# First norm's modulation in a two-layer DiT block: columns in eight buffers, pairs of chunks side by side, reordered loads and weight shares

## The chip, the cores and the metric

The kernel runs on one core of one Trainium2 chip. The metric is the device time of one execution in microseconds (us), as the median of three runs. Engines are called PE (TensorE), DVE (VectorE), ACT (ScalarE), POOL (GpSimd) and SP (SyncE, which here only issues DMAs). Line numbers (L1359) are those of the kernel before, as the profile has them.

## The reference

What is computed is two layers of a transformer block on 256 latent and 256 context tokens of width 1024. Only its start matters here:

```python
mod  = silu(c)     @ w_mod[l] + b_mod[l]      # 6 x 1024 values: sh1, sc1, g1, sh2, sc2, g2
modc = silu(c_ctx) @ w_mod[l] + b_mod[l]      # the same for the context tokens
h  = rms_norm(x,  g_norm1[l]) * (1 + sc1)  + sh1
hc = rms_norm(xc, g_norm1[l]) * (1 + scc1) + shc1
y, yc = token_mixer(h, hc, ...)               # mLSTM, MLA and neighbourhood attention, merged
x = x + g1 * y
x = x + g2 * sqrelu_mlp(rms_norm(x, g_norm2[l]) * (1 + sc2) + sh2, w_ff1[l], w_ff2[l])
```

All is float32. `c` and `c_ctx` are single vectors, so the modulation is a product of a 1024-vector (two of them, latent and context) with a matrix of 1024 x 6144.

## The kernel before

Features lie on the 128 partitions in KC = 8 chunks, the 512 tokens on the free axis. A product in float32 is made as three products of rounded operands: each weight block and each activation is split into a high part (hH, wH, a rounded copy) and a low part (hL, wL, the rest), and PE does high*high, high*low and low*high. ACT makes the high parts of the weights (`high`, L831 to L841), POOL and DVE the low parts. A weight block lies in the ring `raw`, `wH`, `wL`, which has room for two of the 1 MiB blocks `ml`. For a block called shared, DVE does the first 5/8 of the low part (`share_ahead`, L1280 to L1291, 1280 columns) and POOL the last 3/8 (768 columns). Blocks ml 0 and ml 1 are shared.

The order of work is written out by hand: each engine has its own program, which it runs in order, and waits on semaphores. What lies ahead of the first projection:

- **Shift and gate values by DVE.** `mod(m)` (L1293) multiplies rows of w_mod with the broadcast silu(c) and sums along the free axis, four passes of 1024 elements for each 1 MiB of w_mod. The first four (MOD_START = 4) give the shift sh1 of layer 0. Two buffers hold the data, so the load of mod m waits until mod m-2 is done (L571).
- **Scale values by PE.** The scale sc1 of layer 0 is made by `columns(i)` (L2002): for each chunk i of the contraction, 0.5 MiB of w_mod (`p_modk`) is streamed against a stationary operand of two columns (latent, context) into two PSUM banks, rows 0 and 1. Five buffers hold the eight chunks (L392), so chunks 5, 6 and 7 wait until PE has read 0, 1 and 2 (L614). ACT copies the two rows out (L928 to L930, a bank at a time), PE turns them onto the partitions (L2036 to L2041), and DVE adds the bias (L1358 to L1360) and makes the gains (L1320).
- **Tokens.** PE transposes x and ctx (L2021 to L2026), ACT copies them to `x` (L922) and squares them (L889), PE sums the squares with a matrix of ones (L1999), ACT makes 1/rms by Ln and Exp (L901, L902).
- **The norm** (`norm` on DVE, L1323, and on ACT, L897). DVE scales chunks c and c+1 (`scaled`, L1335), ACT adds the shift and rounds (L910, L912), DVE makes the low part of the even chunk (L1344) and POOL that of the odd chunk (L718). DVE's scaling of chunk 5 waits for POOL's low part of chunk 1.
- **The first projection** (`leading`, L1894 to L1913). PE takes each chunk of h as soon as its low part is there, for three groups of weights in ml 0 and ml 1 (9 matmuls of 512 columns a chunk, 72 in all).

ACT's order is: squares, `ahead(-1)` (the high parts of ml 0 and ml 1, L927), the two copies of the scale rows (L928), the DMA that spills x, then Ln and Exp. DVE's order is: mod 0 to 3, `share_ahead(-1)` (its shares of ml 0 and ml 1, L1353), bias of the shift (L1356), the wait for the turned scale rows (L1357), two adds (L1359), two gains (L1320), the norm. SP's order of loads is:

```python
load_mod(0); ctx, x; load_columns(0); load_mod(1); load_columns(1..4)
load_mod(2); ml 0, ml 1; load_columns(5); load_mod(3); load_columns(6), (7); ml 2 ...
```

All these transfers go through one hardware queue, in order. ml 2 takes the place of ml 0, so its load waits for both halves of ml 0's low part (L562, L565).

Of the kernel before, what the change touches and what calls it, by code (L numbers as in the profile page):

```python
# [25 lines left out]
ALU = mybir.AluOpType  # L26
ACT = mybir.ActivationFunctionType
AX = mybir.AxisListType.X

D = 1024  # L30
# [6 lines left out]
P = 128  # L37
KC = D // P
# [19 lines left out]
R_G1, R_G2, R_BMOD, R_GOUT, R_GCQ, R_GCKV, R_GQ, R_GK, R_NGQ, R_NGK = (0, 8, 16, 64, 68, 71, 73, 74, 75, 76)  # L58
# [57 lines left out]
class Steps:  # L116
# [5 lines left out]
    def link(self, instruction):  # L122
        instruction.then_inc(self.sem, 1)
        self.n += 1
        self.eng.wait_ge(self.sem, self.n)
# [198 lines left out]
def build(nc, a, out):  # L324
    ctx = ExitStack()
    with ctx:
# [5 lines left out]
        def S(name):  # L332
            if name not in sems:
                phase, _, what = name.partition("_")
                base, hw = 0, name
                if what and phase[-1].isdigit():
                    kind = phase.rstrip("0123456789")
                    turn = 2 * int(phase[3]) + int(phase[4]) if kind == "nrm" else int(phase[-1])
                    hw = f"{kind}_{what}"
                    base = sum(signals(kind, t)[what] for t in range(turn))  # L340
                if hw not in handles:
                    handles[hw] = ctx.enter_context(nc.semaphore(hw))
                sems[name] = Sem(handles[hw], base)
            return sems[name]
# [14 lines left out]
        par = sb("par", [P, DEPTH, N_ROWS])  # L359
        modT = sb("modT", [P, DEPTH, 48, 2])  # L360
        gain = sb("gain", [P, KC, 2])
        cb = sb("cb", [P, 2, D])
        ccol = sb("ccol", [P, KC, 2])
# [10 lines left out]
        def view(at, *dims):  # L374
            n = int(np.prod(dims))
            v = arena[:, at:at + n]
            if len(dims) == 2:
                return v.rearrange("p (a b) -> p a b", a=dims[0])
            if len(dims) == 3:
                return v.rearrange("p (a b c) -> p a b c", a=dims[0], b=dims[1])  # L380
            return v

        x = view(0, KC, TOK)
        ident = const[:, C_ID:C_ID + P]
        flip = const[:, C_FLIP:C_FLIP + P]
        ones = const[:, C_ONE:C_ONE + P]
        bank = [ctx.enter_context(nc.psum_tensor("bank0", [P, 512], F32))]
# [2 lines left out]
        bank += [ctx.enter_context(nc.psum_tensor(f"bank{b}", [P, 512], F32)) for b in range(3, 8)]  # L390
        m_nd = pair[:, :].rearrange("p (t w) -> p t w", t=NTILE)
        k_raw = [view(at, D) for at in (12288, 13312, 14336, 6144, 7168)]  # L392
        k_row = gst[:, :, :].rearrange("p s t -> p (s t)")
        x_spill = nc.dram_tensor("x_spill", (P, KC, TOK), F32).ap()

# [161 lines left out]
        def _(sp):  # L557
# [10 lines left out]
            def load_mod(m):  # L568

                if m >= 2:  # L570
                    sp.wait_ge(*S("mod_done").at(m - 1))  # L571
                if m == MODS:
                    sp.wait_ge(*S("mg0_low").at(KC))
                l, pair = PAIRS[m]
                src = a["p_mod"][l][2 * pair:2 * pair + 2].rearrange("c p k -> p c k")
                sp.dma_start(mod_raw[:, m % 2, :, :], src).then_inc(S(f"mod_full{m % 2}").handle, 16)
# [31 lines left out]
            def load_all(name, l, js):  # L608
                for j in js:
                    load(name, l, j)  # L610
            def load_columns(i):

                if i >= len(k_raw):
                    sp.wait_ge(*S("k_done").at(i - len(k_raw) + 1))  # L614
                sp.dma_start(k_raw[i % len(k_raw)], a["p_modk"][i]).then_inc(S(f"k_full{i % len(k_raw)}").handle, 16)

            load_mod(0)
            for src, dst in ((a["ctx"], 0), (a["x"], 2)):
                sp.dma_start(xtok[:, dst:dst + 2, :], src[0].rearrange("(t p) d -> p t d", p=P)).then_inc(S("x_in").up(16), 16)
            load_columns(0)  # L620
            load_mod(1)
            for i in range(1, 5):
                load_columns(i)
            load_mod(2)
            load_all("ml", 0, range(2))
            load_columns(5)
            load_mod(3)
            load_columns(6)
            load_columns(7)
            for j in range(2, 7):  # L630
                load("ml", 0, j)
                if MOD_START + j - 2 < MOD_PROJ:
# [152 lines left out]
        def _(act):  # L785
            steps = Steps(act, S("act_step").handle)
            link = steps.link
# [138 lines left out]
                square(0, 0, 0, c)  # L926
            ahead(-1)  # L927
            for b in range(2):  # L928
                act.wait_ge(*(S("k_done").at(KC) if b else S("k_row").at(1)))
                act.activation(k_row[0:2, 512 * b:512 * b + 512], bank[b][0:2, :], ACT.Copy).then_inc(S("k_out").up(1), 1)  # L930
            act.wait_ge(*S("zeroed").at(1))
            for l in range(DEPTH):
                t0 = first_token(l)
# [5 lines left out]
                for j in range(7):  # L939
                    ahead(N["ml", l, j])  # L940
                    for b in range(2):
                        if j == 1:
                            src = full(u0 + j, b)[:, :].rearrange("p (a s t) -> p a s t", a=2, s=2)
                            for i in range(2):
                                for r in range(2):
                                    ins = act.activation(m_k[64 * r:64 * r + 64, 2 * b + i], src[64 * i:64 * i + 64, :, r, :], ACT.Copy)
# [45 lines left out]
                for it in range(2 * ML_H + 2):  # L992
# [4 lines left out]
                    h = it // 2 - 1  # L997
# [10 lines left out]
                for br in ("na", "mla"):  # L1008
# [5 lines left out]
                    if br == "mla":  # L1014
                        act.activation(l_t, small[:, :, 32:64], ACT.Square).then_inc(S(tag + "krs").up(1), 1)
                        exp_and_ln()
                        for j in range(2):
                            for b in range(2):
                                c = 2 * j + b
# [238 lines left out]
        def _(dve):  # L1258
            steps = Steps(dve, S("dve_step").handle)
            link = steps.link  # L1260
# [19 lines left out]
            def share_ahead(n):  # L1280

                while share_at[0] < reach(n):
                    m = share_at[0]
                    share_at[0] += 1
                    if not SHARED[m]:
                        continue
                    cut = cut_chunk(blocks[m][1]) * blocks[m][2]
                    dve.wait_ge(*S("w_high").at(2 * m + 1))
                    dve.tensor_tensor(flat(wL, m)[:, 0:cut], flat(raw, m)[:, 0:cut],
                                      flat(wH, m)[:, 0:cut].bitcast(F32), ALU.subtract)\  # L1290
                        .then_inc(S("w_share").handle, share_step(m))  # L1291
# [31 lines left out]
            def norm(l, which, t0):  # L1323
                tag = f"nrm{l}{which}_"
                sh = M_SH1 if which == 0 else M_SH2
                dve.wait_ge(*S(tag + "std").at(1))
                halves = [(s, lo) for s, lo in ((CTXS, 0), (LAT, CTX)) if lo >= t0]

                def scaled(c):

                    if c >= 4 and c % 2:
                        dve.wait_ge(*S(tag + "lowp").at((c - 3) // 2))
                    for s, lo in halves:
                        r = slice(lo, lo + 256)
                        dve.scalar_tensor_tensor(n_t[:, c % 4, r], x[:, c, r], gain[:, c, s:s + 1], n_std[:, r],  # L1335
                                                 ALU.mult, ALU.mult).then_inc(S(tag + "t").up(1), 1)

                for c in range(0, KC, 2):
                    scaled(c)
                    scaled(c + 1)  # L1340
                    dve.wait_ge(*S(tag + "high").at(len(halves) * (c + 1)))
                    for s, lo in halves:
                        r = slice(lo, lo + 256)
                        ins = dve.scalar_tensor_tensor(hL[:, c, r], n_t[:, c % 4, r], modT[:, l, sh + c, s:s + 1],  # L1344
                                                       hH[:, c, r].bitcast(F32), ALU.add, ALU.subtract)
                    ins.then_inc(S(tag + "lowd").up(1), 1)
# [3 lines left out]
            dve.wait_ge(*S("cb_silu").at(4))  # L1350
            for m in range(MOD_START):
                mod(m)
            share_ahead(-1)  # L1353
            dve.wait_ge(*S("par_in").at(S("par_in").n))
            dve.wait_ge(*S("mod_done").at(MOD_START))
            add_bias(0, 0, 8)  # L1356
            dve.wait_ge(*S("k_turned").at(1))  # L1357
            for s in range(2):  # L1358
                link(dve.tensor_tensor(modT[:, 0, 8:16, s], bank[2][:, 0:16].rearrange("p (c s) -> p c s", s=2)[:, :, s],  # L1359
                                       par[:, 0, R_BMOD + 8:R_BMOD + 16], ALU.add))  # L1360
            gains(0, 0)

            def rope(dst, src, at, tile, groups):
# [14 lines left out]
            for l in range(DEPTH):  # L1378
# [115 lines left out]
                for it in range(2 * ML_H + 3):  # L1494
# [8 lines left out]
                    h = (it - 3) // 2  # L1503
# [263 lines left out]
                for j in range(4):  # L1767
                    for b in range(2):
                        c = 2 * j + b
# [84 lines left out]
        def _(pe):  # L1854
# [146 lines left out]

            def columns(i):  # L2002

                pe.wait_ge(*S(f"k_full{i % len(k_raw)}").at(16 * (i // len(k_raw) + 1)))
                for b in range(2):
                    ins = pe.matmul(bank[b][0:2, :], ccol[:, i, :], k_raw[i % len(k_raw)][:, 512 * b:512 * b + 512],
                                    start=i == 0, stop=i == KC - 1)
                    if b:
                        ins.then_inc(S("k_done").up(1), 1)
                    elif i == KC - 1:  # L2010
                        ins.then_inc(S("k_row").up(1), 1)

            pe.wait_ge(*S("const_in").at(16))
            pe.wait_ge(*S("ccol_silu").at(1))
            for b in range(4):
                for kk in range(4):
                    s, k = b // 2, 4 * (b % 2) + kk
# [8 lines left out]
                ins.then_inc(S("x_cols").up(1), 1)  # L2026
            pe.wait_ge(*S("cb_silu").at(2))
            columns(0)
            columns(1)
            columns(2)  # L2030
            pe.wait_ge(*S("xT_done").at(8))
            for c in range(KC):
                square_sum(0, 0, 0, c)
            for i in range(3, KC):
                columns(i)
            for b in range(2):  # L2036
                pe.wait_ge(*S("k_out").at(b + 1))
                for c in range(4):
                    cc = 4 * b + c
                    ins = pe.transpose(bank[2][:, 2 * cc:2 * cc + 2], k_row[0:2, cc * P:cc * P + P], ident[0:2, 0:2])  # L2040
            ins.then_inc(S("k_turned").up(1), 1)  # L2041
            for l in range(DEPTH):
                t0 = first_token(l)
                tag = f"ml{l}_"
# [31 lines left out]
                for d in range(2):  # L2076
# [3 lines left out]
                    for t in range(NTILE):  # L2080
                        at = (d * 4 + t) * 4
# [327 lines left out]
```

## Time and profile before

| what | value |
|---|---|
| median of 3 runs | 1631.7 us (1631.3, 1631.7, 1633.2) |
| the profiled execution, its own time | 1633.33 us |
| its span, first to last instruction | 1631.6 us |
| PE busy | 1550.2 us, 95% of the span |
| DVE, ACT, POOL busy | 63%, 46%, 43% |
| DMA over the span | 141 GB/s mean, 333 GB/s in the first fortieth (40.8 us) |
| PE busy in the first fortieth | 7 tenths, 9 or 8 tenths nearly everywhere else |

The profile shows one execution, so durations come from it alone; its own time is 1.6 us above the median of the three runs. A busy tenth is an average over 40.8 us. All that the change touches lies in the first 50 us or so. "SPq" and "ACTq" mark the issuing of a DMA by that engine's sequencer; the data land later.

### The profile page before, as it was taken

Reading aid. Unit: us, or ns where it says so; the run is one execution under the profiler, and the core shown is the slowest. Engines: PE = TensorE matmul, PEld = TensorE weight load, DVE = VectorE, ACT = ScalarE, POOL = GpSimd, SP = SyncE. Lnnn points to the kernel's source line nnn. Section 1 sums busy time; section 2 is a strip of 40 time slices with the busy share of each in tenths; the row PEclk is TensorE's granted clock in tenths of the full one; section 3 lists DMA queues with packets and bytes.
Section 4 is the critical chain, followed back from the end, with each engine's and each line's share of the span. In section 5 each row is a group of like instructions: output and inputs, shape, how many; then the busy total and the mean of one; then the engine's idle time right before and its main releaser. Section 6 shows DMA issues by size and latency. Waiting matters only on the chain.

```text
span 1631.6 us, 24934 instructions
## 1 busy us (share of the span) xinstructions
PE 1550.2 (95%) x9698; PEld 1325.1 (81%) x9698; DVE 1025.6 (63%) x1717; ACT 742.7 (46%) x1518; POOL 694.1 (43%) x406
## 2 busy tenths in 40 slices
PE   7899999999999998999999998979998989989998
PEld 3787889867887686788888886968997876989998
DVE  5757946874467764677696956254328387766554
ACT  4434553365545644523232234346436656554442
POOL 0453424624343013545554653474355651334442
PEclk9899999999999999999999998989999999999999
DMA  8443545402234132243454743242431433535553
GB/s 333 175 171 145 181 142 169 176 32 68 72 135 169 29 133 101 74 182 111 171 206 159 281 179 129 72 142 72 142 104 53 133 123 104 182 130 188 186 186 113
DMA packets 69852, 230.64 MB, mean 141 GB/s; under 512 B 18280, under 2 KB 24808, under 8 KB 56424
## 3 DMA queue, kind: packets, MB, share of 16 engines
q1 hardware_dynamic: 60880, 213.67, 37.1%
q10 hardware_dynamic: 8856, 15.39, 2.6%
q8 instruction: 77, 1.26, 0.3%
q14 instruction: 39, 0.32, 0.1%
HBM read 216.45 MB, written 12.58 MB: 140 GB/s over the span
## 4 chain that ended last, share of the span: by engine, by line
PE 73%; DVE 12%; ACT 5%; issue 4%; POOL 3%; DMA 2%; SPq 0%; ACTq 0%; POOLq 0%; DVEq 0%
PE bank L1890 39%; PE bank L1972 9%; PE bank L1928 7%; PE bank L1910 4%; PE bank L1954 3%; PE bank L2291 2%; PE bank L2267 2%; ACT wH L840 2%; PE bank L2278 2%; DVE mjunk L1304 2%; DVE acc L1307 2%; POOL wL L700 1%; PE bank L2141 1%; POOL arena L771 1%; ACT arena L1168 1%
## 5 line engine op out<-in xcount | busy, mean ns | idle before, releaser
L700 POOL TENSOR_TENSOR wL<-raw,wH 128x1280 fp32r<-128x1280 f32 (+2 forms) x144 | 299.0, 2076 | 429.6 <-ACT wH L840 429.4
L702 POOL TENSOR_TENSOR wL<-raw,wH 128x768 fp32r<-128x768 f32 (+3 forms) x198 | 331.1, 1672 | 342.9 <-ACT wH L840 342.8
L840 ACT ACTIVATE wH<-raw 128x768 fp32r<-128x768 f32 (+6 forms) x396 | 297.0, 807 | 393.2 <-PE bank L1890 292.3
L1890 PE MATMUL bank<-hH,wH 128*128 128x512 f32 (+1 forms) x720 | 247.1, 343 | 2.9 <-POOL wL L702 1.5
L1890 PE MATMUL bank<-hH,wL 128*128 128x512 f32 (+1 forms) x720 | 244.8, 340 | 0.0
L1890 PE MATMUL bank<-hL,wH 128*128 128x512 f32 (+1 forms) x720 | 244.8, 340 | 0.0
L1890 PE MATMUL bank<-oH,wH 128*128 128x512 f32 (+1 forms) x576 | 193.9, 337 | 0.5 <-issue 0.5
L1890 PE MATMUL bank<-oH,wL 128*128 128x512 f32 (+1 forms) x576 | 193.8, 336 | 0.0
L1890 PE MATMUL bank<-oL,wH 128*128 128x512 f32 (+1 forms) x576 | 193.8, 336 | 0.0
L1307 DVE SCALAR_TENSOR_TENSOR acc<-acc,cb 128x1024 f32<-128x1024 f32 x88 | 165.6, 1895 | 2.5
L1890 PEld LDWEIGHTS bank<-hH,wH 128*128 128x128 f32 x720 | 136.6, 190 | 20.5 <-POOL wL L702 2.1
L1890 PEld LDWEIGHTS bank<-hL,wH 128*128 128x128 f32 x720 | 136.7, 190 | 15.5 <-issue 0.7
L1890 PEld LDWEIGHTS bank<-hH,wL 128*128 128x128 f32 x720 | 136.6, 190 | 15.0
L1972 PE MATMUL bank<-wH,hH 128*128 128x256 f32 x480 | 137.1, 286 | 3.7 <-POOL wL L702 3.3
L1928 PE MATMUL bank<-hH,wH 128*128 128x512 f32 (+1 forms) x384 | 137.0, 357 | 2.7 <-POOL wL L702 2.0
L1972 PE MATMUL bank<-wH,hL 128*128 128x256 f32 x480 | 136.0, 283 | 0.0
L1972 PE MATMUL bank<-wL,hH 128*128 128x256 f32 x480 | 136.0, 283 | 0.0
L1928 PE MATMUL bank<-hH,wL 128*128 128x512 f32 (+1 forms) x384 | 131.1, 341 | 0.0
L1928 PE MATMUL bank<-hL,wH 128*128 128x512 f32 (+1 forms) x384 | 130.7, 340 | 0.0
L1890 PEld LDWEIGHTS bank<-oH,wH 128*128 128x128 f32 x576 | 109.4, 190 | 12.2 <-issue 1.0
L1890 PEld LDWEIGHTS bank<-oH,wL 128*128 128x128 f32 x576 | 109.4, 190 | 11.2
L1890 PEld LDWEIGHTS bank<-oL,wH 128*128 128x128 f32 x576 | 109.4, 190 | 11.1
(216 smaller groups left out, 3066.8 us busy)
## 6 DMA issues: line engine op xcount, KB each, us to landing
raw<-in_p_ff SPq DMA_DIRECT2D x64, 1024.0 KB, 4.8
acc<-in_p_mod SPq DMA_DIRECT2D x44, 1024.0 KB, 5.5
raw<-in_p_ml SPq DMA_DIRECT2D x12, 1024.0 KB, 5.0
raw<-in_p_na SPq DMA_DIRECT2D x12, 1024.0 KB, 5.3
raw<-in_p_mgc SPq DMA_DIRECT2D x16, 512.0 KB, 3.6
raw<-in_p_mga SPq DMA_DIRECT2D x16, 512.0 KB, 3.8
raw<-in_p_mgb SPq DMA_DIRECT2D x16, 512.0 KB, 3.7
raw<-in_p_out SPq DMA_DIRECT2D x8, 1024.0 KB, 4.8
```

The source lines that it names most:

```text
L700: pool.tensor_tensor(l_[:, 0:cut], r_[:, 0:cut], h_[:, 0:cut].bitcast(F32), ALU.subtract)
L702: pool.tensor_tensor(l_[:, cut:k * w], r_[:, cut:k * w], h_[:, cut:k * w].bitcast(F32), ALU.subtract)\
L840: act.activation(flat(wH, n)[:, part], flat(raw, n)[:, part], ACT.Copy)\
L1304: link(dve.scalar_tensor_tensor(mjunk[:, :], row, 1.0, cb[:, LAT, :], ALU.mult, ALU.mult, accum_out=modT[:, l, chunk, LAT:LAT + 1]))
L1307: ins = dve.scalar_tensor_tensor(row, row, 1.0, cb[:, last, :], ALU.mult, ALU.mult, accum_out=modT[:, l, chunk, last:last + 1])
L1890: ins = pe.matmul(dst, w_[:, kk, c:c + P], r_[:, kk, lo:TOK], start=kk == k0 and m == 0, stop=kk == k0 + kn - 1 and m == 2)
L1910: ins = pe.matmul(dst, w_[:, kk, c:c + P], r_[:, kk, lo:TOK], start=kk == 0 and m == 0, stop=kk == KC - 1 and m == 2)
L1928: ins = pe.matmul(bank[gate_bank(l, T)][:, t0:TOK], w_[:, kk, :], r_[:, kk, t0:TOK], start=kk == 0 and m == 0, stop=kk == KC - 1 and m == 2)
L1954: ins = pe.matmul(bank[2 + T % 2][:, t0:TOK], w_[:, kk, :], r_[:, o + kk, t0:TOK], start=kk == 0 and m == 0, stop=kk == 3 and m == 2)
L1972: ins = pe.matmul(bk[:, o:o + width], s_[:, at[kk], t * P:t * P + P], w_[:, kk, c:c + width], start=kk == 0 and m == 0, stop=kk == k - 1 a ...
L2267: pe.matmul(bank[4 + i][:, 0:nk], l_q[0:MLA_D, 2 * g + i, t * P:t * P + P], l_k[0:MLA_D, 2 * g + i, 0:nk], start=True, stop=True).then_inc ...
L2278: ins = pe.matmul(bank[s % 2][64 * i:64 * i + 64, 0:P], v_[:, c, h * 64:h * 64 + 64], s_pt[:, i, c * P:c * P + P], start=c == 0, stop=c == ...
```

## The change

Three more buffers are given to the columns, in the place where x and ctx lie until PE has transposed them; the load of chunk 5 waits for those transposes and no load of a chunk waits for another chunk. The chunks are multiplied in pairs: the even chunk writes PSUM rows 0 and 1, the odd chunk rows 64 and 65 of the same bank, so each bank holds two partial sums. ACT copies both (four copies in place of two), PE turns both (16 transposes in place of 8, into two banks), and DVE adds both (four adds in place of two). Chunk 4 is loaded behind mod 2, chunks 5, 6 and 7 behind it, then mod 3, then ml 0 and ml 1. DVE does its shares of ml 0 and ml 1 behind the scaling of chunks 0 and 1.

```diff
         k_raw = [view(at, D) for at in (12288, 13312, 14336, 6144, 7168)]
+        k_raw += [view(at, D) for at in (8192, 9216, 10240)]
...
             def load_columns(i):
-                if i >= len(k_raw):
-                    sp.wait_ge(*S("k_done").at(i - len(k_raw) + 1))
-                sp.dma_start(k_raw[i % len(k_raw)], a["p_modk"][i]).then_inc(S(f"k_full{i % len(k_raw)}").handle, 16)
+                if i == 5:
+                    sp.wait_ge(*S("x_cols").at(KC))
+                sp.dma_start(k_raw[i], a["p_modk"][i]).then_inc(S(f"k_full{i}").handle, 16)
...
             load_mod(1)
-            for i in range(1, 5):
+            for i in range(1, 4):
                 load_columns(i)
             load_mod(2)
+            for i in range(4, KC):
+                load_columns(i)
+            load_mod(3)
             load_all("ml", 0, range(2))
-            load_columns(5)
-            load_mod(3)
-            load_columns(6)
-            load_columns(7)
...
             for b in range(2):
-                act.wait_ge(*(S("k_done").at(KC) if b else S("k_row").at(1)))
-                act.activation(k_row[0:2, 512 * b:512 * b + 512], bank[b][0:2, :], ACT.Copy).then_inc(S("k_out").up(1), 1)
+                act.wait_ge(*S(("k_row", "k_done")[b]).at(1))
+                for h in range(2):
+                    r = slice(64 * h, 64 * h + 2)
+                    ins = act.activation(k_row[r, 512 * b:512 * b + 512], bank[b][r, :], ACT.Copy)
+                ins.then_inc(S("k_out").up(1), 1)
...
                     scaled(c)
                     scaled(c + 1)
+                    if (l, which, c) == (0, 0, 0):
+                        share_ahead(-1)
...
             for m in range(MOD_START):
                 mod(m)
-            share_ahead(-1)
...
-            dve.wait_ge(*S("k_turned").at(1))
-            for s in range(2):
-                link(dve.tensor_tensor(modT[:, 0, 8:16, s], bank[2][:, 0:16].rearrange("p (c s) -> p c s", s=2)[:, :, s],
-                                       par[:, 0, R_BMOD + 8:R_BMOD + 16], ALU.add))
+            dve.wait_ge(*S("k_turned").at(2))
+            for h in range(2):
+                for s in range(2):
+                    link(dve.tensor_tensor(modT[:, 0, 8:16, s], bank[2 + h][:, 0:16].rearrange("p (c s) -> p c s", s=2)[:, :, s],
+                                           modT[:, 0, 8:16, s] if h else par[:, 0, R_BMOD + 8:R_BMOD + 16], ALU.add))
...
             def columns(i):
-                pe.wait_ge(*S(f"k_full{i % len(k_raw)}").at(16 * (i // len(k_raw) + 1)))
+                for h in range(2):
+                    pe.wait_ge(*S(f"k_full{i + h}").at(16))
                 for b in range(2):
-                    ins = pe.matmul(bank[b][0:2, :], ccol[:, i, :], k_raw[i % len(k_raw)][:, 512 * b:512 * b + 512],
-                                    start=i == 0, stop=i == KC - 1)
-                    if b:
-                        ins.then_inc(S("k_done").up(1), 1)
-                    elif i == KC - 1:
-                        ins.then_inc(S("k_row").up(1), 1)
+                    for h in range(2):
+                        ins = pe.matmul(bank[b][64 * h:64 * h + 2, :], ccol[:, i + h, :], k_raw[i + h][:, 512 * b:512 * b + 512],
+                                        start=i == 0, stop=i == KC - 2)
+                    if i == KC - 2:
+                        ins.then_inc(S(("k_row", "k_done")[b]).up(1), 1)
...
             columns(0)
-            columns(1)
             columns(2)
             pe.wait_ge(*S("xT_done").at(8))
             for c in range(KC):
                 square_sum(0, 0, 0, c)
-            for i in range(3, KC):
-                columns(i)
+            columns(4)
+            columns(6)
             for b in range(2):
                 pe.wait_ge(*S("k_out").at(b + 1))
                 for c in range(4):
                     cc = 4 * b + c
-                    ins = pe.transpose(bank[2][:, 2 * cc:2 * cc + 2], k_row[0:2, cc * P:cc * P + P], ident[0:2, 0:2])
-            ins.then_inc(S("k_turned").up(1), 1)
+                    for h in range(2):
+                        r = slice(64 * h, 64 * h + 2)
+                        ins = pe.transpose(bank[2 + h][:, 2 * cc:2 * cc + 2], k_row[r, cc * P:cc * P + P], ident[r, 64 * h:64 * h + 2])
+                        if (b, c) == (1, 3):
+                            ins.then_inc(S("k_turned").up(1), 1)
```

## Rows read from the trace of the kernel before

**Rows 1.** Chain that ended last, first 100 us: start, duration (us), what.

```profile
23.92 10.66 DMA acc<-in_p_mod
...
46.05 4.18 PE bank L1910 x9
...
50.27 14.75 PE bank L1910 x60
...
65.12 1.28 ACT wH L840
```

**Rows 2.** Timeline of DVE, 34 to 46 us: start, duration, engine line op, tiles, [idle before].

```profile
34.60 1.23 DVE L1304 SCALAR_TENSOR_TENSOR mjunk<-acc,cb 128x1024 f32<-128x1024 f32 x1 [5.23 <-DMA acc<-in_p_mod]
...
39.43 2.89 DVE L1289 TENSOR_TENSOR wL<-raw,wH 128x1280 fp32r<-128x1280 f32 x2
42.24 0.36 DVE L1313 TENSOR_TENSOR modT<-modT,par 128x8 f32<-128x8 f32 x2
42.64 0.37 DVE L1359 TENSOR_TENSOR modT<-bank,par 128x8 f32<-128x8 f32 x2
43.04 0.37 DVE L1320 SCALAR_TENSOR_TENSOR gain<-modT,par 128x8 f32<-128x8 f32 x2
43.44 1.67 DVE L1335 SCALAR_TENSOR_TENSOR arena<-arena,gain 128x256 f32<-128x256 f32 x4
```

**Rows 3.** Timeline of ACT, 28 to 42 us.

```profile
28.21 3.88 ACT L840 ACTIVATE wH<-raw 128x1280 fp32r<-128x1280 f32 x4
...
39.52 0.59 ACT L930 ACTIVATE gst<-bank 2x512 f32<-2x512 f32 x1 [0.27 <-PE bank L2006]
...
40.01 0.66 ACT L901 ACTIVATE arena<-bank,eps 128x512 f32<-128x512 f32 x1
```

**Rows 4.** Timeline of PE, 20 to 41 us.

```profile
21.95 7.53 PE L1999 MATMUL bank<-arena,const 128*128 128x512 f32 x16
...
35.88 3.60 PE L2006 MATMUL bank<-arena,ccol 128*2 128x512 f32 x8 [1.16 <-DMA arena<-in_p_modk]
...
40.16 0.40 PE L2040 MATMUL bank<-const,gst 2*128 2x2 f32 x4 [0.34 <-ACT gst L930]
```

**Rows 5.** Load lines, one short window each: chunks 2 and 3, then 6 and 7 (L615).

```profile
L615 SPq DMA_DIRECT2D arena<-in_p_modk x2: 503/504/504, 4.1 to 4.6; - x2
...
DMA to landing us min/median/max: 15.2/15.6/16.0
...
L615 SPq DMA_DIRECT2D arena<-in_p_modk x2: 430/448/467, 24.3 to 24.9; - x2
...
DMA to landing us min/median/max: 11.5/11.9/12.2
```

**Rows 6.** The same for ml 0 and ml 1, then ml 2 (L566).

```profile
L566 SPq DMA_DIRECT2D raw<-in_p_ml x2: 432/450/468, 19.3 to 19.8; - x2
...
DMA to landing us min/median/max: 7.6/8.6/9.6
...
L566 SPq DMA_DIRECT2D raw<-in_p_ml x1: 327/327/327, 41.0 to 41.0; - x1
...
DMA to landing us min/median/max: 9.3/9.3/9.3
```

**Rows 7.** The same for mod 2 (L576).

```profile
L576 SPq DMA_DIRECT2D acc<-in_p_mod x1: 378/378/378, 18.9 to 18.9; - x1
...
DMA to landing us min/median/max: 5.5/5.5/5.5
```

**Rows 8.** Timeline of POOL and DVE in the norm, 46 to 54 us.

```profile
46.54 4.90 POOL L718 TENSOR_TENSOR hL<-arena,hH 128x512 fp32r<-128x512 f32 x2 [12.58 <-ACT arena L912]
...
50.25 1.88 DVE L1335 SCALAR_TENSOR_TENSOR arena<-arena,gain 128x256 f32<-128x256 f32 x2 [1.17 <-POOL hL L718]
...
53.55 1.31 POOL L718 TENSOR_TENSOR hL<-arena,hH 128x512 fp32r<-128x512 f32 x1 [2.10 <-ACT arena L912]
```

**Rows 9.** Busy time of each engine in a stretch; then PEclk, DMA share, GB/s.

```profile
46.00:51.00 5.00, 4.91 (x11) 3.45 (x12) 3.83 (x9) 3.66 (x10) 4.46 (x2) 0.50 0.97 393
```

## The prediction

> **What bounds the kernel now.** PE is busy 95% of the span, and the change is worth what it does to the moment at which PE enters that long busy stretch. I read the chain of waits first [rows 1]: PE's first projection starts at 46.05 us, and from 50.27 its matmuls run without a hole. Ahead of it the chain goes back over DVE to the load of mod 3, issued at 23.92 and landed 10.66 us later, at 34.58. The timelines show the steps between [rows 2]: DVE does mod 3 from 34.60 to 39.43, its shares of ml 0 and ml 1 until 42.24 (2.8 us), bias, adds and gains (0.4 us a pair, each add 0.2), and starts the norm at 43.44. I call this moment N. PE starts 2.6 us after it (46.05 - 43.44). The scale rows were not the bound: ACT's last copy ended at 40.11 [rows 3] and the turning at 40.56 [rows 4], 2.1 us ahead of DVE's first use of them at 42.64. Loads are one steady stream: ml 0 landed at 19.3 + 7.6 = 26.9 and ml 1 at 19.8 + 9.6 = 29.4 [rows 6], so 2.5 us for 1 MiB; the last of the twelve MiB, chunk 7, landed at 24.9 + 12.2 = 37.1 [rows 5].
>
> **The change part by part.**
>
> *Loads.* The bytes are the same, the order is not. Behind mod 3 there was 1 MiB (chunks 6 and 7); now there are 2 MiB (ml 0 and ml 1). So mod 3 lands 5 us before the end of the stream, about 32.1 in place of 34.6. But ml 1 is now last: it lands at the end of the stream, about 37.1, in place of 29.4. The end itself has bounds. At its pace the stream would need 6.3 us for the 2.5 MiB behind ml 1 and end at 35.7; it took until 37.1, and that surplus may or may not come back. On the other side there may be a hole: chunk 3 landed at 4.6 + 16.0 = 20.6 [rows 5], mod 2 is issued at 18.9 [rows 7], and chunk 4 no longer stands between them. Mod 2 took 5.5 us from issue to landing for 2.5 us of data, so at most 3.0 us pass before its first data; chunk 3's data cover 1.7 of them, and the hole is 0 to 1.3 us. So ml 1 lands between 35.7 and 38.4; I take 37.5, the measured end with a third of the hole.
>
> *ACT.* Its program still has the high parts of ml 0 and ml 1 ahead of the scale rows. Before, they ran from 28.21 [rows 3], in time that ACT had to spare. Now ACT sits at ml 0 and ml 1 until their data are there, and behind this wait are queued the copies of the scale rows, the spill's DMA, Ln and Exp; PE's transposes, DVE's adds and the whole norm wait for those. A block's high parts take 3.88 / 2 = 1.94 us, so ACT is free at 37.5 + 2.0 = 39.5. Four copies follow at a pitch of 0.5 (39.52 to 40.01 in rows 3), in place of one open copy at the end before: done at 41.5. Ln takes 0.66 from 40.01 [rows 3] and Exp is one like it, so both end some 1.2 us behind the last copy: 42.7. Turning eight pieces at 0.1 us each [rows 4] ends at 42.4, four adds at 0.2 at 43.2, gains at 43.6 [rows 2]. So N is 43.6, 0.2 us later than before, though mod 3 is done at 32.1 + 4.9 = 37.0 and DVE now stands idle for some 5 us.
>
> *Shares.* They leave DVE's stretch ahead of N, where they would by now be free, and stand between the scaling of chunks 0 and 1 and the low part of chunk 0, for which PE waits: 42.24 - 39.43 = 2.8 us on the path. PE's start is N + 2.6 + 2.8 = 49.0. PE also needs POOL's low part of chunk 1. Before, it was ready at N + 6.8 (PE went on at 50.27), though POOL had its data at 46.54: two such operations took 4.90 us there while one alone takes 1.31 [rows 8], so POOL got through only when DVE stopped, at its own wait for POOL. The shares push that stop by the same 2.8 us. From chunk 1 on, PE is the slower one as before. So PE's whole program moves by 0.2 + 2.8 = 3.0 us.
>
> *PE's columns.* They are covered. Two chunks one after the other took 3.60 us [rows 4]. If pairs don't overlap at all: four chunks from about 18 to 25, the squares' sums 7.5 us to 32.7, four chunks 7.2 us to 39.9, with the first bank done earlier; ACT wants the first bank at 39.5. If they overlap fully, PE is done by 36. Either way ACT is not held up by more than a few tenths; if the cover went (ACT free earlier), the first case would cost up to the difference.
>
> *Buffers, waits of SP.* Chunk 5's wait for the transposes costs nothing: they end before mod 2 is issued. ml 2's load, before at 41.0, now waits for the share of ml 0, until about N + 3.1 = 46.7; with its 9.3 us to landing [rows 6] it is there at 56, ahead of 65.12 + 3, when ACT first wants it [rows 1]. mod 4 and the blocks behind it move alike. POOL's own part of ml 1's low part (before N in both kernels) is done at about 41.3. Cost nothing.
>
> *Sum.* +0.2 (N) and +2.8 (shares) = +3.0 us. The profiled execution took 1633.33, so it would take 1636.3; against the median of 1631.7 that is 1634.7. The terms are differences, so the 1.6 us between the two executions stays out of them.
>
> **A rule against the row.** POOL's and DVE's operations exclude each other in rows 8: 4.90 us for two against 1.31 for one, and DVE's two at 50.25 took 1.88, where four take 1.67 in rows 2. In my sum POOL finds no opening between the two shares. The Trainium skill, SBUF — State Buffer, section "SBUF: two separate sides", says that whichever of a DVE operation with two SBUF inputs and a GpSimd operation starts first holds the shared ports for its whole instruction. By that rule the boundary between the shares may go to POOL, which is a rival below; the trace agrees with the exclusion but has no such boundary.
>
> **The rivals.**
>
> *A: POOL gets in between the shares, or the clock stays low longer (slower by more than 0.2%).* POOL's data for chunk 1 are there at N + 3.1, and the first share ends at N + 3.1 too. If POOL takes the ports there, the second share, chunk 0's low part and PE's start come 1.2 us later, while PE's short wait for chunk 1 (0.2 to 0.3 us) goes: +3.9 to +4.0, 1635.7. For it speaks the coincidence, against it that POOL, ready at 46.54, got in at no boundary of DVE's until that stopped at 50.25 - 1.17 = 49.1 [rows 8]. PE's clock adds to it: it was granted 0.50 (1.2 GHz) over 46 to 51 us [rows 9], after 5.5 us with nothing for PE to do. Five us at half speed cost 2.5; a stretch half as long again costs 1.2 more, a shorter one gives as much back.
>
> *B: the stream ends early.* If ml 1 lands at 35.7, N is 41.8 and the shift is 2.8 - 1.6 = +1.2: 1632.9.
>
> *C: ACT is not in the way (faster).* Were the scale rows copied before the high parts of ml 1, DVE's own path would set N: mod 3 done at 37.0, then 0.4 + 0.8 + 0.4: 38.6. PE starts 5.4 later, at 44.0, and the kernel is 2.0 us faster, 1629.7. It decides as soon as ACT has its copies done before 37.5. Against it stands ACT's written order, and that ml 1's bytes come last. Even this is not 0.2% faster.
>
> *D: the pairs are not side by side.* PE's columns end near 39.9, and up to 0.4 us is added: within the forecast.
>
> **How the numbers follow.** About 0.2% (3.3 us) is what a measurement of this kernel can tell from no change. The forecast, +3.0 (its own range +2.4 to +3.9, by a landing between 36.9 and 38.4), has 57%, D in it; A 24%; B 13%; C 4%; the rest, something that neither shows, 2%. Faster by over 0.2%: 4%, part of C with a shorter slow stretch of the clock. Slower by over 0.2%: A and a quarter of the forecast, 38%. Within: 58%. The range goes from just under B, 1632.4, to A with a longer slow stretch, 1637.0.
>
> **What would show each step.** In the changed profile ACT idles until about 37.5 for ml 1's data, and four copies of L930's kind follow at about 39.5; DVE is idle from about 37 until near 42.5 (for PE's turning); the two shares lie between the scalings and the first low part; PE's first projection starts at about 49.0, and chunk 1 some 4 us later. Mod 3 starts near 32. Wrong it would be if the copies lie ahead of 37, if PE starts ahead of 47.5, or if the shift at the start is not found again at the end.

## The result and the profile after

Slower. The first four executions of the changed kernel had a median of 1640.2 us against 1631.9 for the kernel before: ratio 1.0048, interval [1.0035, 1.0061], 8.3 us. Two later runs put it lower: 1.0032 [1.0020, 1.0044] and 1.0027 [1.0015, 1.0040], both 5 us above a median of 1632.5. The 15 executions together have a median of 1637.9. The profiled one took 1637.89, 4.6 us more than the profiled one of before. I forecast +3.0 us (1634.7), with a range up to 1637.0; the time of 1640.2 lies above it.

Chain of waits of the changed kernel, first 100 us (start, duration, what):

```profile
25.38 12.95 DMA raw<-in_p_ml
38.34 0.02 issue
38.36 0.38 ACT wH L840
...
46.31 2.80 DVE wL L1292 x2
49.11 1.81 DVE hL L1349 x2
50.92 0.14 issue
51.06 18.57 PE bank L1915 x69
```

The chain no longer goes over mod 3 but over the weights ml 1, which land at 38.3. PE's first projection starts at 51.06, 5.0 us later than in [rows 1]. Timelines of ACT and PE, 35 to 44 us ("gst" is the tile that holds the copied scale rows, "bank" is PSUM):

```profile
35.91 2.00 ACT L840 ACTIVATE wH<-raw 128x1280 fp32r<-128x1280 f32 x2 [7.10 <-DMA raw<-in_p_ml]
...
38.36 1.27 ACT L840 ACTIVATE wH<-raw 128x1280 fp32r<-128x1280 f32 x1 [0.44 <-DMA raw<-in_p_ml]
...
40.27 2.38 ACT L932 ACTIVATE gst<-bank 2x512 f32<-2x512 f32 x4
...
41.49 0.59 PE L2046 MATMUL bank<-const,gst 2*128 2x2 f32 x8 [7.97 <-ACT gst L932]
```

ACT idles 7.1 us for ml 0, again for ml 1, and only then copies the scale rows, whose last matmul PE had finished at 33.5: PE waits 7.97 us for them. These answer to [rows 3, 4]. Timelines of DVE and POOL, 33 to 51 us, which answer to [rows 2, 8] (L1292 are the two shares, L1338 the scalings, L1349 DVE's low part of chunk 0, L718 POOL's of chunk 1):

```profile
33.43 1.22 DVE L1307 SCALAR_TENSOR_TENSOR mjunk<-acc,cb 128x1024 f32<-128x1024 f32 x1 [3.99 <-DMA acc<-in_p_mod]
...
38.44 1.78 DVE L1316 TENSOR_TENSOR modT<-modT,par 128x8 f32<-128x8 f32 x2
...
43.42 0.37 DVE L1364 TENSOR_TENSOR modT<-bank,par 128x8 f32<-128x8 f32 x2 [3.20 <-PE bank L2046]
...
44.64 1.67 DVE L1338 SCALAR_TENSOR_TENSOR arena<-arena,gain 128x256 f32<-128x256 f32 x4
...
46.23 2.89 DVE L1292 TENSOR_TENSOR wL<-raw,wH 128x1280 fp32r<-128x1280 f32 x2
...
47.73 2.50 POOL L718 TENSOR_TENSOR hL<-arena,hH 128x512 fp32r<-128x512 f32 x1 [5.49 <-ACT arena L912]
...
49.03 1.88 DVE L1349 SCALAR_TENSOR_TENSOR hL<-arena,modT,hH 128x256 fp32r<-128x256 f32 x2
```

Mod 3 comes 1.2 us earlier than in [rows 2] and buys nothing: DVE waits 3.2 us for the turned rows, the norm starts at 44.64, the shares follow, and then DVE's low part of chunk 0 takes 1.88 us in place of 0.88. POOL's operation was issued at 47.73 and ended at 50.23; one alone takes 1.3 [rows 8], so it ran from about 49 on, from the end of the second share, and DVE stood for 1.0 us behind it. PE then finds chunk 1 ready, so its wait of 0.24 us there is gone.

Part of this comes from the loads. Stretches of 1 us, first one of the kernel before, then three of the changed kernel (columns: stretch, length, busy time of PE, PEld, DVE, ACT, POOL, PEclk, DMA share, GB/s):

```profile
20.00:21.00 1.00, 1.00 (x3) 0.17 (x2) 0.96 (x3) 0.31 (x1) 0.00 (x0) 1.00 1.04 418
```

```profile
19.00:20.00 1.00, 1.00 (x6) 0.07 (x2) 0.90 (x3) 0.99 (x2) 0.00 (x0) 1.00 0.88 348
20.00:21.00 1.00, 0.35 (x2) 0.12 (x4) 0.96 (x3) 0.84 (x2) 0.00 (x0) 1.00 0.62 82
21.00:22.00 1.00, 1.00 (x8) 0.18 (x4) 1.00 (x3) 0.00 (x0) 0.00 (x0) 1.00 0.71 270
```

In these 3 us 0.70 MB moved, where the kernel before moved 1.24 MB, so the stream lost 1.3 us. This is the hole that the prediction had as possible: mod 2's load is issued at 19.43, when the data ahead of it are nearly through, and the stream is back at full pace 2 us later. Mod 3 and ml 1 both land late by it: 33.4 and 38.3, where the prediction's sum without a hole gives 32.1 and 37.1.

From PE's start on, these two traces stay in step: DVE's first instruction behind the projection lies 4.6 us later (69.05 for 64.43), and the same matmuls lie 3.9 to 4.7 us later up to the last. The two other profiles of the changed kernel, with PE's start 4.5 and 4.7 us later, begin their last long stretch of matmuls 6.5 and 6.8 us later than the profile of before. One profile against one can't tell such a difference from the spread of the executions (below).

### The profile page after: what moved, and what is told of

It is laid out like the page before. It is cut to its first block, busy times and chain, and to the rows that moved or that the text cites. A ratio compares the mean times of both kernels' runs of the same rounds, so it can differ in the third digit from the quotient of the medians.

```text
span 1636.2 us, 24957 instructions
## 1 busy us (share of the span) xinstructions
PE 1544.1 (94%) x9706; PEld 1325.0 (81%) x9706; DVE 1027.9 (63%) x1719; ACT 744.7 (46%) x1520; POOL 693.1 (42%) x406
## 3 DMA queue, kind: packets, MB, share of 16 engines
q1 hardware_dynamic: 60880, 213.67, 37.1%
## 4 chain that ended last, share of the span: by engine, by line
PE 75%; DVE 12%; ACT 4%; issue 3%; POOL 3%; DMA 2%; SPq 1%; ACTq 0%; POOLq 0%; DVEq 0%
PE bank L1895 39%; PE bank L1977 9%; PE bank L1933 7%; PE bank L1915 5%; PE bank L1959 3%; PE bank L2298 2%; PE bank L2274 2%; PE bank L2285 2%; ACT wH L840 2%; DVE mjunk L1307 2%; DVE acc L1310 1%; POOL wL L700 1%; PE bank L2148 1%; DMA raw<-in_p_ml 1%; POOL arena L771 1%
```

## The experiments

Each run was timed beside the kernel before. I read each in two ways: by PE's start (46.05 before, 51.06 changed), which comes from one profiled execution and varies by 0.5 us between the three profiles of the changed kernel, and by the median, which varies by a microsecond or two.

**The changed kernel again**, twice, no edit.

> The changed kernel once more, nothing edited, for what its profile doesn't explain: profile against profile it is 4.6 us slower, median against median 8.3. Clock theory: the executions differ in how long PE runs at half speed (granted clock 0.976 in the profiled one, 0.974 to 0.975 in the others, which is some 3 us of half-speed time each thousandth); expects the spans of this run to fall on levels some 1.7 us apart, the longer with the lower granted clock. Rival, the load stream: the weights land later in the longer executions, the clock no different; expects no relation of span and clock.

> The changed kernel a third time, for the size of its loss, which the first runs put at 8.3 us (four executions) and the second at 5.0 (five). My theory (all of the loss is PE's later start, 4.5 to 5.0 us in the two profiles, the rest is the spread that the kernel before shows as well): 5 us over the kernel before, ratio 1.003, PE at 50.5 to 51.1. Rival (something later costs 2 to 3 us more): ratio 1.0045 or more.

Medians 1637.49 and 1637.35, PE's start 50.56 and 50.70. The 5 us stand; the 8.3 us of the first four executions are not found again, and why those four were longer stays open. PE's later start gives 4.5 to 5.0 us of it. The two intervals, together 2.4 to 7.2 us, neither show nor exclude a further microsecond or two from later in the program.

**The kernel before, as a run of its own.**

> The kernel before as a run of its own, for its spans and granted clocks. Clock theory: 1631.5 to 1633.5, and the longer ones have the lower clock (0.979 in the profiled one of 1633.3). Load theory: spread without a relation to the clock.

Twelve executions from 1630.64 to 1636.45, ratio 1.0001 [0.9993, 1.0010]. The fastest four had a granted clock of 0.980 to 0.982, the slowest four of 0.978 to 0.980; the changed kernel's were 0.977 to 0.978 in its fastest and 0.975 in its slowest executions of the last run. The clock theory holds as a tendency, without clean levels. Between the two kernels the mean clock says little: in the changed one PE does no more than the turning from 33.5 to 51.06, the clock is at 0.50 from 36.5 to about 56.5, some 20 us, where it was at 0.50 from 42 to 52 before, and 10 us more at half speed in 1636 are the 0.003 between 0.979 and 0.976. Nearly all of these 10 us are idle. What the theory is made of can be seen in two profiles of one kernel. Stretches of the kernel before, first its own profile, then this run's (columns: stretch, length, busy time of PE, PEld, DVE, ACT, POOL, PEclk, DMA share, GB/s):

```profile
46.00:49.00 3.00, 2.95 (x7) 2.40 (x8) 3.00 (x8) 3.00 (x9) 2.46 (x1) 0.50 0.94 384
49.00:52.00 3.00, 2.97 (x7) 1.86 (x7) 1.83 (x3) 0.90 (x3) 2.44 (x2) 0.50 1.03 423
```

```profile
46.00:49.00 3.00, 2.95 (x7) 2.40 (x8) 3.00 (x8) 3.00 (x9) 2.46 (x1) 0.50 0.95 381
49.00:52.00 3.00, 2.58 (x10) 1.73 (x10) 1.83 (x3) 0.88 (x3) 2.46 (x2) 0.96 1.03 422
```

All engines are in step until about 49 us. Then the clock is back at 0.96 in one and still at 0.50 (1.2 GHz) in the other, and PE does 10 matmuls against 7 in 3 us. Such differences move an execution by 1 to 3 us on its way: the same stretch of matmuls starts 0.8 us earlier in the second profile at 71 us (70.48 for 71.28) and 2.4 us earlier at 240, and 0.6 us later at 1456. That the clock is behind all of these is not shown. One profile or four executions can't tell 3 us from 6.

**Shares back to their old place** in the changed kernel.

```diff
             for m in range(MOD_START):
                 mod(m)
+            share_ahead(-1)
...
-                    if (l, which, c) == (0, 0, 0):
-                        share_ahead(-1)
```

> The changed kernel with DVE's two shares of the weights again behind mod 3 and ahead of the bias. There DVE waits for the scale rows in the changed profile (about 40.2 to 43.4 us), so the shares should be hidden: norm start unchanged at 44.6, PE's first projection at 47.3 in place of 51.1. My theory (shares on the path, 2.8 us, and 1.0 us in which POOL takes the ports from DVE's low part): 3.6 us faster than the changed kernel, about 1636.6. Rival (the loss is all in the scale rows behind ACT's weights, the shares were hidden by something later, such as POOL's low part of chunk 1): no more than 1 us faster.

Median 1635.75, ratio 1.0019 [1.0010, 1.0027]; norm start 45.81 in place of 44.6, PE at 48.42. So 2.6 us of PE's start come back where I had 3.8. The term was right in kind, but the shares were not fully hidden. DVE and POOL of that run, 37 to 45 us:

```profile
37.92 2.00 POOL L702 TENSOR_TENSOR wL<-raw,wH 128x768 fp32r<-128x768 f32 x1 [37.04 <-ACT wH L840]
38.18 6.11 DVE L1292 TENSOR_TENSOR wL<-raw,wH 128x1280 fp32r<-128x1280 f32 x2
```

Two shares take 6.11 us where they take 2.89 in [rows 2]: they meet POOL's own parts of the same blocks.

**Copies of the scale rows first.** ACT's loop over the copies moved ahead of `ahead(-1)`.

```diff
-            ahead(-1)
             for b in range(2):
                 act.wait_ge(*S(("k_row", "k_done")[b]).at(1))
...
+            ahead(-1)
```

> The changed kernel with ACT's copies of the scale rows ahead of the high parts of ml 0 and ml 1; Ln and Exp stay behind them. My theory (ACT's order sets the norm's start): the rows are turned by 37, the norm starts when Exp is done, about 41.8 in place of 44.6, PE at 48.2; 2.9 us faster than the changed kernel, about 1637.3. Rival (DVE's mods or the loads set the start): no change within 0.5 us.

Norm start 41.86, PE at 48.28, as expected (41.8, 48.2); median 1635.72, ratio 1.0021 [1.0009, 1.0033], 1.8 us below the changed kernel. ACT's order is worth 2.8 us of PE's start. That the norm start came out to a tenth is in part luck: I had Exp as its bound, but Exp ended at 41.10, and DVE's two small gains took 1.41 us in place of 0.37, because POOL was making its low part of ml 1 until 41.60.

**POOL waits for DVE's first low part** in the changed kernel.

```diff
                     pool.wait_ge(*S(tag + "high").at((2 if t0 == 0 else 1) * (c + 1)))
+                    if (l, which, c) == (0, 0, 1):
+                        pool.wait_ge(*S(tag + "lowd").at(1))
```

> The changed kernel, with POOL's low part of chunk 1 held back until DVE has made that of chunk 0, which takes the 1.0 us away that POOL holds the ports ahead of it. My theory (exclusive ports, taken at the boundary behind the shares): DVE's low part of chunk 0 takes 0.9 in place of 1.9 us and PE starts 1.0 us earlier than in the changed kernel; POOL then gets in only when DVE stops, so chunk 1 is ready at norm start + 9.7, and about 0.5 us of the 1.0 is left. Rival (the 1.9 us is not POOL's doing, such as a late high part): PE's start doesn't move.

```profile
45.05 1.67 DVE L1340 SCALAR_TENSOR_TENSOR arena<-arena,gain 128x256 f32<-128x256 f32 x4
...
49.45 0.87 DVE L1351 SCALAR_TENSOR_TENSOR hL<-arena,modT,hH 128x256 fp32r<-128x256 f32 x2
...
50.46 0.77 PE L1917 MATMUL bank<-hH,wH 128*128 128x512 f32 x1 [6.76 <-DVE hL L1351]
```

In this timeline DVE's low part takes 0.87 us, and PE starts 5.4 us after the norm in place of 6.4. So the 1.0 us was POOL's hold of the ports. The norm itself started 0.4 us later here, so PE's start gained 0.6 us. Median 1635.27, ratio 1.0020 [1.0011, 1.0029]; that it gains 2 us and not 0.5 is not explained; the intervals of the two ratios overlap.

**The three parts of the change, each alone on the kernel before.** Loads: eight buffers and the new order. Pairs: eight buffers, pairs, old order of loads, shares in their old place. Shares: moved behind the first scalings.

```diff
             for m in range(MOD_START):
                 mod(m)
-            share_ahead(-1)
...
                     scaled(c + 1)
+                    if (l, which, c) == (0, 0, 0):
+                        share_ahead(-1)
```

> The kernel before with the eight buffers and the new order of loads only: single columns, two copies, shares in their old place. My theory (ml 1 last in the stream holds ACT's copies back until 40.4, and the shares, no longer with their data in time, run against POOL's low parts): mod 3 starts at 33.4, the shares end about 44.2 as in the run with shares back, norm start 45.4, PE at 48.0; 2 us slower than the kernel before. Rival (the earlier mod 3 pays): PE at 45 or before, 1 us faster.

> Eight buffers and pairs of chunks side by side, but the old order of loads and the shares in their old place. My theory (the scale rows had 2.1 us of slack in the kernel before, pairs change only what is behind them): two more adds, norm start at 43.8, PE at 46.5, 0.4 us slower than before. Rival (four copies in place of two use up the slack, or the pairs shorten the path): norm start at 44.5 or later, or at 43.0 or earlier.

> The kernel before with one edit: DVE's two shares behind the first scalings. Five buffers, old loads, single columns. My theory (the move takes 2.8 us from ahead of the norm's start, of which the scale rows, turned at 40.6, let 2.0 through, and puts 2.8 on PE's start, and 1.0 for POOL's hold of the ports): norm start 41.4, PE at 47.8, 1.7 us slower than before. Rival (the move only swaps two steps of DVE and is even): PE at 46 to 46.8.

| part alone | norm start | PE's start | against 46.05 | ratio, interval |
|---|---|---|---|---|
| loads | 45.16 | 47.77 | +1.7 | 1.0021 [1.0011, 1.0030] |
| pairs | 44.31 | 46.92 | +0.9 | 1.0003 [0.9994, 1.0012] |
| shares | 41.64 | 48.06 | +2.0 | 1.0009 [1.0001, 1.0018] |

No part gains, and the three add up to 4.6, near the 5.0 of the whole. That sum is no proof: in the run of the loads the scale rows were turned at 41.5 and DVE used them at 44.35, so the norm waited there for the shares (6.10 us for two, against POOL's parts), while in the whole change it waits for ACT. Loads and shares came out as my theory had them, within 0.3 us. Pairs cost 0.9 in place of 0.4. The two extra adds are 0.4 of it, as expected, and mod 3 landed 0.5 us later than before; DVE went through to the norm without a wait for PE. What I had not thought of is PE's part, and it used up slack only. PE in that run, 32 to 48 us:

```profile
32.61 1.89 PE L2013 MATMUL bank<-arena,ccol 128*2 128x512 f32 x8 [2.52 <-DMA arena<-in_p_modk]
37.66 3.43 PE L2013 MATMUL bank<-arena,ccol 128*2 128x512 f32 x8 [3.16 <-DMA arena<-in_p_modk]
```

and the stretch of the second row:

```profile
37.00:41.00 4.00, 3.34 (x8) 0.40 (x8) 3.97 (x7) 1.17 (x2) 0.00 (x0) 0.57 0.00 0
```

A pair at full clock takes 1.89 us, half of [rows 4]'s 3.60 for two chunks: side by side works. But PE, now fast, waits longer for data, and for the last pair the granted clock was 0.57: 3.43 us, nearly as long as two single chunks. The scale rows were turned at 42.8, 0.3 us ahead of DVE's first use of them, where the kernel before had 2.1. The 0.5 us of mod 3 go with a later issue of mod 2 in this execution (20.04 in place of 18.90) and a hole of 0.7 us behind it; it is not shown that the pairs cause it.

**Shares in the gap ahead of mod 3**, on the kernel before.

```diff
             for m in range(MOD_START):
+                if m == 3:
+                    share_ahead(-1)
                 mod(m)
-            share_ahead(-1)
```

> The kernel before, in its old order of loads, with DVE's two shares ahead of mod 3 instead of behind it. ACT has the high parts done at 32.1 us and DVE idles from 29.4 to 34.6 for mod 3's data, so the shares should cost nothing there. My theory (what counts is DVE's work behind the landing of mod 3): mod 3 still starts at 34.6, the norm starts when the scale rows and Exp are there, 41.4, PE at 44.0 in place of 46.05: 2.0 us faster than the kernel before, about 1630.5. Rival (POOL's own low parts hold the ports in the gap and push the shares into mod 3): 0 to 1 us faster.

PE at 45.04, 1.0 us earlier, half of what I expected; median 1631.24, ratio 0.9998 [0.9990, 1.0007], no change that can be measured. Here the rival had a point. DVE and POOL, 30 to 37 us:

```profile
30.95 5.39 POOL L702 TENSOR_TENSOR wL<-raw,wH 128x768 fp32r<-128x768 f32 x2 [30.07 <-ACT wH L840]
...
34.76 2.67 DVE L1304 SCALAR_TENSOR_TENSOR mjunk<-acc,cb 128x1024 f32<-128x1024 f32 x1
```

The four low parts exclude each other, the gap is too short for them, and mod 3's first pass takes 2.67 us in place of 1.23.

**ACT's high part of ml 0 two squares earlier**, on top of that.

```diff
             for c in range(KC):
+                if c == 6:
+                    high(0)
+                    high_at[0] = 1
                 square(0, 0, 0, c)
```

> The kernel before with the shares ahead of mod 3, and ACT's high part of ml 0 ahead of the last two squares (ml 0 has landed at 27), so that DVE's and POOL's low parts, which exclude each other, start 1.5 us earlier and are done by mod 3's landing. My theory: mod 3's passes run at 1.2 us each again, norm start 41.4 in place of 42.4, PE at 44.0, 2 us faster than the kernel before. Rival (POOL still holds the ports at 34.6, or the later squares hold back PE's columns 3 to 5 and with them the scale rows): PE at 45 or later.

PE at 44.81, 0.8 us short of the aim; median 1632.92, ratio 1.0003 [0.9994, 1.0012]. Mod 3's passes are back at 1.2 us but start at 35.5, and the scale rows, held back by the later squares, are turned at 41.3, 0.7 us later than before. Both halves of the rival came true in small.

**All of ACT's norm work first**, and POOL waiting, on the changed kernel: copies, spill, Ln and Exp ahead of `ahead(-1)`.

```diff
+            act.dma_start(x_spill[:, :, 0:], x[:, :, 0:]).then_inc(S("spilled").handle, 16)
+            root_mean(0, 0, 0)
             ahead(-1)
             for l in range(DEPTH):
                 t0 = first_token(l)
-                act.dma_start(x_spill[:, :, t0:], x[:, :, t0:]).then_inc(S("spilled").handle, 16)
+                if l:
+                    act.dma_start(x_spill[:, :, t0:], x[:, :, t0:]).then_inc(S("spilled").handle, 16)
```

> The changed kernel with all of ACT's work for the norm (scale rows, spill, Ln, Exp) ahead of the weights' high parts, and POOL's first low part of the norm behind DVE's. My theory (the new order's losses are ACT's order, 2.8 us, the ports, 1.0, and the shares, 2.8): norm start about 40.5 to 41, shares behind the first scalings done at 45.4, PE at 46.3, about equal to the kernel before (1632.3): the earlier mod 3 just pays for the shares. Rival (the shares behind the scalings are no loss once ACT's order is right): PE at 44 or before, 2 us faster than the kernel before.

The norm starts at 40.65, as expected, 4 us ahead of the changed kernel's. Yet PE starts at 47.61, not 46.3, and the median is 1635.98, ratio 1.0026 [1.0016, 1.0037]. The spill of x (2 MiB) is now issued at 33.7, while the last weights are under way, and ml 1 lands at 40.0; and the norm meets POOL's part of ml 1:

```profile
40.04 2.00 ACT L842 ACTIVATE wH<-raw 128x1280 fp32r<-128x1280 f32 x2 [1.53 <-DMA raw<-in_p_ml]
...
42.12 4.66 POOL L702 TENSOR_TENSOR wL<-raw,wH 128x768 fp32r<-128x768 f32 x1 [1.73 <-ACT wH L842]
...
45.05 2.42 DVE L1359 SCALAR_TENSOR_TENSOR hL<-arena,modT,hH 128x256 fp32r<-128x256 f32 x2
```

No version beats the kernel before by what can be measured.

## Why the prediction was wrong

- **The main mechanism was right.** ACT's in-order wait for ml 0 and ml 1 stands ahead of the scale rows: expected idle until 37.5, seen until 38.3, and worth 2.8 us of PE's start by the run with the copies first. The shares on the path cost 2.8 us (46.31 to 49.11 in the chain). The shift is made before PE's start, and in the two profiles shown it is kept to the end.
- **The step that failed is the sum's N, +0.2 us taken.** It is +1.2 in the first profile, +0.7 and +0.8 in the two others. Two terms were mis-sized. ml 1 landed at 38.3 (37.8 and 38.0 in the others) where I took 37.5: I had bounded the hole by 1.3 us rightly and then took a third of it without a reason, and the traces show 1.3, 0.8 and 0.9 us. The four copies took 2.38 us where I took 4 x 0.5, a pitch of 0.60. My 0.5 came from a copy followed by Ln; but in the run of the loads alone two copies of rows 0 and 1 took 1.04 us together, so it isn't the kind of the next operation. The copies of the changed kernel alternate between rows 0 and 64; whether that is the reason is not shown. Turning took 0.6 us, not 0.8.
- **Rival A's 1.0 us was real and belonged in the sum.** I had given POOL the boundary between the two shares, with 24% for A as a whole. POOL had its data at 47.73, 0.1 us after the second share had started (47.63), in the profile shown and likewise in the four others with the shares there and POOL free, so the boundary that I priced was over by a tenth. It took the next one, behind the second share, where DVE's low part of chunk 0 follows. My ground for excluding an opening, that POOL had got in at no boundary before, came from a run of DVE's own scalings and low parts and did not carry over to the shares. This happened in all three profiles of the changed kernel, with the copies first and with the shares alone (1.88 us each time). The exclusion itself is as the Trainium skill, SBUF — State Buffer, section "SBUF: two separate sides", has it: the trace agrees, 1.88 us against 0.87 once POOL is held back. Which of two that wait gets the ports, that section doesn't say for our case, and no run here settles it: between two shares POOL got in with the shares back in their place (3.09 us a share), and was passed over with ACT's work first (1.48 a share), waiting in both. The other half of A did not happen: behind PE's start the clock stayed at 0.50 for 5.5 us, before for 5.9.
- **The sum by what was measured:** 1.2 + 2.8 + 1.0 = 5.0 for PE's start, less 0.2 to 0.3 for the wait on chunk 1, 4.7 against 4.6 seen. On the profiled 1633.33 that is 1638.0 (1637.89 measured). It leaves 3.6 us of the 8.3 between the first medians without a cause; the later runs didn't find them again. With the 5 us that they found, the time would have been 1636.7, inside the range, so that it fell outside is as much the spread of those four executions as the two terms.
- **The range was too narrow at the top.** It added A to the forecast but not A to a late landing, and it took the spread of the median of three to be small, where single executions of one kernel differ by 6 us.
- **Covered, as predicted:** PE's columns (done at 33.5), chunk 5's wait, the later load of ml 2. The hole in the stream is shown: the later DVE is done with mod 0, the later mod 2 is issued and ml 1 lands, 18.68 and 37.8, 18.86 and 38.0, 19.43 and 38.3, and 19.92 and 38.8 in the run where POOL waits (the run with the copies first, 18.95 and 37.7, is 0.3 out of line). In the old order chunk 4 stood in between; with mod 2 issued at 18.90 its stream has no hole (418 GB/s in the row above).

## What to carry to other kernels

When a transfer on the critical chain is moved forward, look at what is now last in the stream and which engine, in its own fixed order, stands in front of that data: the work queued behind the wait may be the new critical chain. An operation that filled an idle stretch costs nothing there and its full length at the head of a pipeline. Where two engines share ports, a step of one that is moved also moves the points at which the other gets in.

## What the runs showed of the hardware

Pairs of products with two columns each, written to rows 0 and 64 of a bank, overlap fully in float32: 1.89 us against 3.60 for the same eight matmuls, both at a granted clock of 1.00. The copies don't: two rows of 512 cost ACT 0.59 us each time, as much as 128 rows of 512 (0.60, ACT's copies at 10 to 13 us in the kernel before), so two partial sums double them. A tiny operation is held as long as a large one: DVE's two adds of 128x8 took 1.78 us in place of 0.36 [rows 2] while POOL made a low part (37.99 to 39.99). A load issued at 19.43, with the stream ahead of it nearly through, had the stream at full pace again only 2 us later, which cost 1.3 us of transfers. And PE's granted clock came back at different times in two executions that were in step until then, and the longer executions of a kernel tended to have the lower mean clock.
